# Gathering expert tokens from two 4-byte parts instead of three bf16 parts

## The reference, cut to what matters

```
scores = sigmoid(t @ w_router);  sel = scores + e_bias
... (only the 4 best of 8 groups of experts stay in sel)
_, eidx = lax.top_k(sel, TOP_K)                      # 8 of 64
w = take_along_axis(scores, eidx);  w = w / sum(w) * 2.5
hg = einsum('cd,edf->cef', xc, w_eg);  hu = einsum('cd,edf->cef', xc, w_eu)
a  = silu(hg) * hu * gates[..., None]
routed = einsum('cef,efd->cd', a, w_ed)
shared = (silu(t @ w_sg) * (t @ w_su)) @ w_sd
```

## Time and profile before

| | |
|---|---|
| median of 3 runs | 1138.94 us |
| the profiled execution | 1141.19 us |
| its span | 1139.4 us |
| TensorE busy | 1086.8 us (95%), 7070 instructions |
| weight loads | 749.6 us (66%) |
| VectorE, ScalarE busy | 381.0 us (33%), 274.0 us (24%) |
| bytes moved | 334.45 MB, mean 294 GB/s |

### The profile page before, as it was taken

One profiled execution on the slowest core, in us unless ns is written; L12 is line 12 of the kernel. 1 busy time (PEld: TensorE's weight loads), 2 busy tenths in 40 slices (PEclk: granted clock), 3 DMA queues, 4 the chain that ended last, 5 costly groups with the idle time before them and its releaser, 6 DMA issues.

```text
span 1139.4 us, 17633 instructions
## 1 busy us (share of the span) xinstructions
PE 1086.8 (95%) x7070; PEld 749.6 (66%) x7070; DVE 381.0 (33%) x975; ACT 274.0 (24%) x614; POOL 52.7 (5%) x85
## 2 busy tenths in 40 slices
PE   6999999999999999999899999999699999999998
PEld 4786875688755455555555556544278888887567
DVE  1398966442613111111121121112033111341941
ACT  2124135501511111112111110111023121212951
POOL 0000202104000000000000000000001001100001
PEclk9999999999999999999999999999799999999999
DMA  9999378945689999999999999999964344210000
GB/s 387 345 421 422 123 322 349 418 160 188 246 304 414 414 416 417 416 416 421 416 420 415 416 419 413 414 418 415 415 276 146 111 144 151 74 38 1 1 1 37
DMA packets 59074, 334.45 MB, mean 294 GB/s; under 512 B 6608, under 2 KB 7984, under 8 KB 28784
## 3 DMA queue, kind: packets, MB, share of 16 engines
q1 hardware_dynamic: 56592, 327.97, 71.4%
q10 hardware_dynamic: 2176, 3.37, 1.0%
q0 software_dynamic: 224, 1.97, 0.4%
HBM read 332.23 MB, written 1.05 MB: 293 GB/s over the span
## 4 chain that ended last, share of the span: by engine, by line
PE 78%; DMA 12%; DVE 4%; SPq 3%; issue 2%; ACT 1%; DVEq 0%; ACTq 0%
DMA ring<-experts 12%; PE bank L1036 11%; PE bank L523 10%; PE bank L1080 5%; PE bank L1171 5%; PE bank L987 4%; PE bank L905 4%; PE bank L430 3%; PE bank L926 3%; PE bank L1272 2%; PE bank L815 2%; PE bank L1223 2%; PE bank L830 2%; PE bank L653 2%; PE bank L589 2%; PE bank L961 2%
## 5 line engine op out<-in xcount | busy, mean ns | idle before, releaser
L1036 PE MATMUL bank<-ring,arena 128*32 128x512 f32 (+1 forms) x1120 | 182.2, 625 | 20.2 <-DMA ring<-experts 19.9
L1036 PEld LDWEIGHTS bank<-ring,arena 128*32 128x32 f32 (+1 forms) x1120 | 53.0, 124 | 131.0 <-issue 130.8
L523 PE MATMUL bank<-hT,ring 128*128 128x256 f32 x576 | 126.9, 381 | 0.0
L523 PEld LDWEIGHTS bank<-hT,ring 128*128 128x128 f32 x576 | 109.0, 190 | 18.2 <-issue 4.0
L1080 PE MATMUL bank<-ring,arena 128*32 128x512 f32 (+1 forms) x560 | 87.6, 597 | 1.7 <-DMA ring<-experts 1.7
L905 PE MATMUL bank<-arena 128*128 128x128 bf16 x1152 | 72.2, 219 | 1.1 <-ACT arena L1632 1.1
L905 PEld LDWEIGHTS bank<-arena 128*128 128x128 bf16 x1152 | 66.9, 98 | 7.9 <-issue 5.0
L2247 DVE TENSOR_TENSOR yhalf<-bank,yhalf 128x512 fp32r<-128x512 f32 x48 | 33.2, 692 | 92.0 <-ACT yhalf L1659 92.0
L2234 DVE SCALAR_TENSOR_TENSOR arena<-bank,arena 128x256 f32<-128x256 f32 x24 | 11.6, 484 | 151.1 <-ACT arena L1651 147.1
L1403 POOL TENSOR_TENSOR hT<-hT 128x256 f32<-128x256 f32 x30 | 21.7, 724 | 852.4 <-ACT hT L1460 851.0
L1171 PE MATMUL bank<-hT,ring 128*128 128x256 f32 x256 | 57.1, 379 | 0.0
(11 more groups left out here) (372 smaller groups left out, 1462.4 us busy)
## 6 DMA issues: line engine op xcount, KB each, us to landing
ring<-stream SPq DMA_DIRECT2D x118, 1024.0 KB, 12.0
ring<-experts SPq DMA_DIRECT2D x114, 1024.0 KB, 17.1
ring<-experts SPq DMA_DIRECT2D x156, 512.0 KB, 14.8
arena<-consts POOLq DMA_DIRECT2D x1, 1664.0 KB, 12.1
resid<-x SPq DMA_DIRECT2D x1, 1024.0 KB, 5.0
resid<-ctx ACTq DMA_DIRECT2D x1, 1024.0 KB, 10.1
arena<-stream SPq DMA_DIRECT2D x1, 1024.0 KB, 11.4
bias_room<-rpb ACTq DMA_DIRECT2D x2, 438.0 KB, 5.5
```

What stands on the lines that cost most here:

```text
L523: mm = mmul(o[:, 0:n_tok], w[:, k, t * P:(t + 1) * P], hT[:, k, 0:n_tok], start=(k == 0), stop=(k == KT - 1))
L1036: mm = mmul(o[at:at + n_slots, :], xg[:, kk, at:at + n_slots], w[g][:, k, :], start=(kk == 0), stop=(kk == KT - 1))
```

## The change

The tokens are split in two parts in the 4-byte single-pass format (`hparts`): ScalarE writes the first from PSUM, VectorE the difference. `htok`, the second and third parts are gone. The gather has 8 x 2 x 2 = 32 instructions a unit. `choose` writes the choice twice, as bf16 (for the gate and scatter products) and as F32R (`chosen_r`). VectorE computes ranks and the sorted list directly after the mask, then the two last rests, then the gates; `ordered` is signalled by the copy itself. TensorE does 5 of 8 k-steps of the first `shu` tile ahead of the sorted list, the others and the second tile behind it and ahead of `by_expert`. The sorted list uses bank 7 instead of 3, the second `shu` tile bank 5 instead of 1. To make room, the first 4096 columns of the arena become a room of their own that is used by early tiles, then by `hparts`, `chosen_r`, `yhalf` and `selT`, then by late tiles.

```diff
+        with nc.sbuf_tensor("early_room", [P, FRONT + 512 + 8 * RUN + 1024], F32) as early_room:
...
+        with nc.sbuf_tensor("hparts", [P, 2, 2, 1024], F32R) as hparts:
+            pass
+        late_room = sb("late_room", [P, FRONT])
...
+        chosen_r = sb("chosen_r", [P, 2, 2, P], F32R)
...
-            shu_tile(0, 6)
+            shu_part(0, 6, range(0, 5))
             pe.wait_ge(S("perm_made"), 1)
-            o = open_group("order", 3)
+            o = open_group("order", 7)
             mmul(o[0:1, 0:64], cc("expert")[0:64, :], perm, start=True, stop=True)
             close_group(mmul(o[0:1, 64:128], count_col, perm, start=True, stop=True), "order")
+            shu_part(0, 6, range(5, KT))
+            shu_part(1, 5, range(KT))
+            slab_end[nu] = ("shu", 1)
             pe.wait_ge(S("gates_made"), 1)
-            done(pe, "pos")
             o = open_group("by_expert", 2)
...
-            shu_tile(1, 1)
-            slab_end[nu] = ("shu", 1)
 
             def gather(m, half):
 
                 o = open_group(("xg", m, half), 4)
                 if half == 0:
                     pe.wait_ge(S("chosen_made"), m + 1)
+                if m == 0:
+                    done(pe, ("tk", half))
+                    done(pe, ("tk", 2 + half))
                 for d in range(4 * half, 4 * half + 4):
                     for t in range(TT):
-                        for q in range(3):
-                            mm = mmul(o[:, P * (d % 4):P * (d % 4) + P], hbf[:, q, t, P * d:P * d + P],
-                                      chosen[m % 2][:, t, :], start=(t == 0 and q == 0), stop=(t == 1 and q == 2))
+                        for q in range(2):
+                            mm = mmul(o[:, P * (d % 4):P * (d % 4) + P], hparts[:, q, t, P * d:P * d + P],
+                                      chosen_r[:, m % 2, t, :], start=(t == 0 and q == 0), stop=(t == 1 and q == 1))
...
             def first_part(gg):
                 full(act, ("tk", gg))
-                a.copy(hbf[:, 0, gg // 2, 512 * (gg % 2):512 * (gg % 2) + 512], bk(("tk", gg))[:, :]).then_inc(S("part_a"), 1)
-
-            def second_part(gg):
-                act.wait_ge(S("rest_a"), gg + 1)
-                a.copy(hbf[:, 1, gg // 2, 512 * (gg % 2):512 * (gg % 2) + 512], htok[:, gg % 2, :]).then_inc(S("part_b"), 1)
+                a.copy(hparts[:, 0, gg // 2, 512 * (gg % 2):512 * (gg % 2) + 512], bk(("tk", gg))[:, :]).then_inc(S("part_a"), 1)
...
             def rest_of(gg):
                 dve.wait_ge(S("part_a"), gg + 1)
-                v.tensor_tensor(htok[:, gg % 2, :], bk(("tk", gg))[:, :], hbf[:, 0, gg // 2, 512 * (gg % 2):512 * (gg % 2) + 512],
-                                ALU.subtract).then_inc(S("rest_a"), 1)
-
-            def third_part(gg):
-                dve.wait_ge(S("part_b"), gg + 1)
-                at = hbf[:, :, gg // 2, 512 * (gg % 2):512 * (gg % 2) + 512]
-                emptied(v.tensor_tensor(at[:, 2, :], htok[:, gg % 2, :], at[:, 1, :], ALU.subtract), ("tk", gg))
+                at = hparts[:, :, gg // 2, 512 * (gg % 2):512 * (gg % 2) + 512]
+                emptied(v.tensor_tensor(at[:, 1, :], bk(("tk", gg))[:, :], at[:, 0, :].bitcast(F32), ALU.subtract), ("tk", gg))
...
-            link(v.tensor_tensor(gates, lg, mask, ALU.mult))
-            link(v.tensor_reduce(den[:, 2:4], gates, AXX, ALU.add))
...
-            for gg in range(2):
-                third_part(gg)
-                done(dve, ("tk", gg))
-                rest_of(gg + 2)
-            third_part(2)
-            third_part(3)
+            link(v.memset(order[0:1, E:E + 1], 0))
+            v.tensor_tensor(gates, lg, mask, ALU.mult)
             full(dve, "pos")
...
+                for to in (chosen[m % 2], chosen_r[:, m % 2]):
+                    if kind == "X":
...
             choose(0)
             full(dve, "order")
-            link(v.memset(order[0:1, E:E + 1], 0))
-            v.tensor_copy(order[0:1, 0:E], bk("order")[0:1, 0:64])
+            v.tensor_copy(order[0:1, 0:E], bk("order")[0:1, 0:64]).then_inc(S("ordered"), 1)
             emptied(v.tensor_copy(count_rank, bk("order")[0:1, 64:128]), "order")
-            done(dve, "order")
-            signal("ordered")
+            rest_of(2)
+            rest_of(3)
+            link(v.tensor_reduce(den[:, 2:4], gates, AXX, ALU.add))
...
```

More of the change, by code:

```diff
@@ L150, in build, with cut @@
         rstd = sb("rstd", [P, 512])
[L151 to L155, removed]
+        arena = sb("arena", [P, ARENA - FRONT])
+        def cut(room, at, n, dims, parts=P):
+            v = room[0:parts, at:at + n]
             if len(dims) == 2:
@@ L160, in ar, with early, late @@
             return v
+        def ar(at, n, *dims, parts=P):
+            return cut(arena, at - FRONT, n, dims, parts)
+        with nc.sbuf_tensor("early_room", [P, FRONT + 512 + 8 * RUN + 1024], F32) as early_room:
+            def early(at, n, *dims):
+                return cut(early_room, at, n, dims)
+            stat = early(FRONT, 512)
+            braw = early(FRONT + 512, 8 * RUN, 8, RUN)
+            bmask = early(FRONT + 512 + 8 * RUN, 1024, 2, 512)
+            wr = early(FRONT + 512, 512, 8, 64)
+        with nc.sbuf_tensor("hparts", [P, 2, 2, 1024], F32R) as hparts:
+            pass
+        late_room = sb("late_room", [P, FRONT])
+        def late(at, n, *dims):
+            return cut(late_room, at, n, dims)
+        chosen_r = sb("chosen_r", [P, 2, 2, P], F32R)
+        yhalf = sb("yhalf", [P, 2, 1024], F32R)
+        selT = sb("selT", [P, 2, P], F32R)
+        sb("rest_of_early_room", [P, 8 * RUN + 1536 - 2816])
         def cc(name, a=0, b=None):
@@ L169, in vv @@
             return ve[:, lo + a:(hi if b is None else lo + b)]
-        qk = ar(0, 2048, 8, 256)
-        vna = ar(2048, 1024, 2, 512)
-        lat = ar(3072, 1024, 4, 256)
+        qk = early(0, 2048, 8, 256)
+        vna = early(2048, 1024, 2, 512)
+        lat = early(3072, 1024, 4, 256)
         sgate = ar(4096, 4096, 16, 256)
@@ L281, in build @@
         rt2 = ar(9216, 1024, 4, 256)
-        outs = ar(0, 2048, 2, 1024)
+        outs = late(0, 2048, 2, 1024)
         gdiag = hT[:, :, T:T + P]
[L285 to L290, removed]
         bank = [ctx.enter_context(nc.psum_tensor(f"bank{b}", [P, 512], F32)) for b in range(8)]
@@ L1102, in more_tokens @@
                         for t in range(TT):
-                            for q in range(3):
-                                mm = mmul(bank[4][:, P * (d % 4):P * (d % 4) + P], hbf[:, q, t, P * d:P * d + P],
-                                          chosen[0][:, t, :], start=(t == 0 and q == 0), stop=(t == 1 and q == 2))
+                            for q in range(2):
+                                mm = mmul(bank[4][:, P * (d % 4):P * (d % 4) + P], hparts[:, q, t, P * d:P * d + P],
+                                          chosen_r[:, 0, t, :], start=(t == 0 and q == 0), stop=(t == 1 and q == 1))
                     mm.then_inc(S("more_on_tensor"), 1)
@@ L2138, in choose @@
                 kind, ranks_of = UNITS[m]
[L2139 to L2149 removed]
+                for to in (chosen[m % 2], chosen_r[:, m % 2]):
+                    if kind == "X":
+                        for r, at, n_slots in ((ranks_of[0], 0, 96), (ranks_of[1], 96, 32)):
+                            src = ranked[:, :, r:r + 1]
+                            last = v.tensor_tensor(to[:, :, at:at + n_slots], bc(cc("iota"), [0, 2], [1, n_slots]),
+                                                   bc(src, [src.ap[1][0], 2], [0, n_slots]), ALU.is_equal)
+                    else:
+                        G = len(ranks_of)
+                        W = P // G
+                        src = ranked[:, :, ranks_of[0]:ranks_of[0] + G] if m else first2
+                        last = v.tensor_tensor(to.rearrange("p t (g w) -> p t g w", g=G), bc(cc("iota"), [0, 2], [0, G], [1, W]),
+                                               bc(src, [src.ap[1][0], 2], [1, G], [0, W]), ALU.is_equal)
                 last.then_inc(S("chosen_made"), 1)
@@ L2153, in _ @@
             full(dve, "order")
-            link(v.memset(order[0:1, E:E + 1], 0))
-            v.tensor_copy(order[0:1, 0:E], bk("order")[0:1, 0:64])
+            v.tensor_copy(order[0:1, 0:E], bk("order")[0:1, 0:64]).then_inc(S("ordered"), 1)
             emptied(v.tensor_copy(count_rank, bk("order")[0:1, 64:128]), "order")
-            done(dve, "order")
-            signal("ordered")
+            rest_of(2)
+            rest_of(3)
+            link(v.tensor_reduce(den[:, 2:4], gates, AXX, ALU.add))
+            link(v.reciprocal(den[:, 2:4], den[:, 2:4]))
+            for t in range(TT):
+                last = v.tensor_scalar(gates[:, t, :], gates[:, t, :], den[:, 2 + t:3 + t], 2.5, ALU.mult, ALU.mult)
+            last.then_inc(S("gates_made"), 1)
             full(dve, "by_expert")
```

44 lines of the change are left out of this document (13 added, 31 removed).

## The result

The changed kernel took 1145.96 us, the median of 3 runs (1145.64 to 1146.42), against 1138.94 before. The ratio is 1.0057, with a 95% interval of 1.0039 to 1.0076. It is slower, by 7.0 us or 0.6%, where 1.7 us were forecast. Its profiled execution took 1145.64 us 4.45 more than the profiled one of before; its span is 1143.8 for 1139.4. In a later session, with 10 runs of the changed kernel and 31 of the one before, the ratio was 1.0034 (1.0017 to 1.0050).

A forecast was written before the change was run, and what follows sets the result against it. The transfer stream, full from 359.5 to 838 us, was taken to set the expert stage's end. Work ahead of unit 0, -0.83, and three gathers, +2.55, gave +1.7 us: 1140.7 us, range 1136.5 to 1151 for 8 in 10.

The forecast's parts named there:

- The gather: Each unit's gather on TensorE: 32 4-byte instructions at 0.110 us for 48 bf16 at 0.056, +0.85 us a unit.
- loads and streams in turn: Rival for the gather: 4-byte loads and streams don't overlap, up to 0.166 us an instruction, 1148 to 1175; chance 0.17.
- two passes: Rival for the gather: two loads a product, 0.22 us each, +78 us, about 1217; chance 0.09.
- a price per instruction: Rival for the gather: load hidden, 0.056 us an instruction, -0.88 us a unit, 1135.5; chance 0.10.
- Ahead of unit 0: Reordered work before the first gather: TensorE starts that gather at 308.14 instead of 308.97, -0.83 us.
- The first restart: Transfer stream's restart at 335.57, after two units' gathers: -0.83 + 2 x 0.85 = +0.9 us.
- The second restart: Transfer stream's restart at 358.57, after three units' gathers: -0.83 + 3 x 0.85 = +1.7 us, all counted.
- The head start: Four slabs asked for 2.5 us sooner through the earlier order; only lengthens the pause at 332.5, priced 0.
- that rival: The early order pays: the 2.5 us head start survives the pause at 332.5, 1136.4 to 1138.2; chance 0.09.
- After 359.5: Expert stage's 21 remaining gathers: +17.9 us of TensorE's work, covered by its waits; the last slab still ends the stage.
- The reserve: TensorE's waits over the rest of the expert stage, about 21.6 us, taken as cover for the later gathers.
- VectorE and the overlays: Second choice, 0.4 to 0.5 us a unit on VectorE, hidden by a 2.68 us wait; overlays add nothing: 0.

The follow-up runs named there:

- The filled kernel: Changed kernel with three k-steps of the shared expert's second up tile between the first gather's halves; 1141.08 us, and 1141.01 us when run again.
- the order alone, e1: Kernel before, three bf16 parts and 48 instructions kept, with only the changed order of work ahead of unit 0; 1139.33 us, ratio 0.9996.
- after_again: The changed kernel unaltered, run again in a later session; 1144.94 us, ratio 1.0034 to the kernel before.
- e3: Changed kernel with units 3 to 23 gathered from the first part alone, units 0 to 2 unchanged; 1141.75 us, ratio 1.0022.
- e2: Changed kernel with units 0 to 2 gathered from the first part alone, 16 instructions each instead of 32; 1138.34 us, ratio 0.9977.
- e4_fill: Changed kernel with three k-steps of the shared expert's second up tile between the first gather's halves; 1141.08 us, ratio 1.0016.
- e4_fill_again: The e4_fill kernel run a second time, no edit; 1141.01 us, ratio 1.0008.
- e10: The e4_fill kernel with all context steps half a unit later; 1158.63 us, ratio 1.0170.
- e6: The e1 kernel with the first part added a second time, so 64 bf16 gather instructions a unit; 1141.94 us, ratio 1.0013.
- e5: The e1 kernel with three k-steps of the shared product between the first gather's halves; 1140.23 us, ratio 0.9997.
- e7: The e5 kernel with all context steps one unit later, none left in unit 0; 1142.64 us, ratio 1.0016.
- e9: The e5 kernel with all context steps half a unit later; 1154.23 us, ratio 1.0112.

## Why the prediction was right and wrong

The mechanism was right as far as it went: slower gathers, covered by the waits behind the restart and paid ahead of it. 1145.96 lies in the range of 1136.5 to 1151, but that is partly luck. The forecast's own 1139.5 to 1142.5 was missed, the value of 1140.7 was 5.3 us too low, and the range went up to 1151 for a dearer gather, which did not come. What brought the time up there was a fall of the clock that the sum did not have. By its steps:

- **The gather.** 0.110 us an instruction was forecast, 0.112 is the median distance of starts; 32 x 0.112 - 2.67 = +0.91 us a unit for +0.85. The loads last 192 ns (188 to 192 said), a half 1.97 to 2.10 us. The rivals of loads and streams in turn (from 0.116 on), of two passes (0.22) and of a price per instruction (0.056) are all out. The row to trust was L787, the 4-byte loads alone. The Trainium skill, TensorE: Matmul & The Clock Gate, section "LDWEIGHTS (loading the stationary operand)", puts a load at its columns over 1.2 in ns, 107 for 128. The 0.112 from start to start agrees within 5% for this format, the 0.056 of the bf16 gather does not; a single load's record is longer in both, 192 and 98 ns.
- **Ahead of unit 0.** -0.83 was forecast, -0.66 came. TensorE did not wait for the permutation, the counts start at 300.96 for 303.34 on VectorE, and the first ordered issue comes 2.4 us earlier.
- **The first restart.** +0.9 was forecast, +4.65 came. The step that failed is not a wait or a price but the clock in unit 0: 6.8 us at 1.2 GHz, 3.4 us lost. The prediction looked at the granted clock only behind long waits at the end of the stage and took unit 0's products at their old duration. The filled kernel, twice, gives 4.4 us back and keeps the gathers; what remains, +0.24, is -0.66 + 1.82 - 0.77 = +0.39 within 0.15.
- **The second restart.** The sum counted three gathers, because the transfers had run low at 357. It should have counted two. In ten traces the last down product follows the first restart by 478.3 to 480.3 us. After against before it is 4.08 us later against the router, with the first issue 4.65 and the second 5.5 later. That alone lies within the spread of 2.0 us. The rates decide: at the second issue the stream moves 324 GB/s for 417 over 2.5 us before and 376 over 5 us after, so it loses an estimated 0.6 and 0.5 us there, as much in one kernel as in the other. By the same steps with two gathers and the measured price, -0.66 + 1.82 = +1.2 was the sum to make, and the clock's 3.4 the term that was missing. The third gather, 0.85 too much in the sum, hid a part of that.
- **The head start** was priced at 0, and in the order alone the issues come 2.4 us earlier and the restart 0.2. Right; that rival is out.
- **After 359.5.** The reserve took the 21 gathers: 7.8 us of waits are left (3 to 8 said), 4.02 of them at the last gate and up products, where 2.3 was said. With 37.6 us of TensorE's work taken away, the last down product moved by 0.7.
- **VectorE and the overlays** were priced at 0. VectorE is busy 386.5 us for 381.0, and TensorE has no wait for it from 303 to 842 us.

The 4.4 us between the spans of the profiled executions are all accounted for: the router 0.42 later, the restart 4.65, what follows it -0.57, the rest -0.10. The medians are 7.0 us apart in the first session and 5.2 in the later one. The profiled execution of before was 2.25 us above its median and the changed kernel's 0.32 below, which is the difference to 7.0; single executions of before lie between 1137.4 and 1144.0. The intervals of both ratios, 1.0039 to 1.0076 and 1.0017 to 1.0050, hold 4.45 us (the first at its lower end), so no loss beyond it is shown.

## What to carry to other kernels

When a transfer stream is the bound, find the last point at which it stood still: only TensorE's work ahead of that point is paid. A dip behind it is no such point when the stream loses little there (0.5 us here). When instructions are replaced by fewer and slower ones, price them by a row of the same load, and then read the granted clock of the stretch behind them, as sparse products with a wait of one microsecond between them may halve it for what comes next. A few independent products moved into that wait are worth more than the wait itself: 4.4 us for 0.98 here.

## What the runs showed of the hardware that was not expected

**The clock fell with TensorE busy.** The granted clock at 312 to 322 us, over all thirteen traces:

```
gather                       wait between its halves   clock
4-byte, 0.112 us each        0.98 us                   1.2 GHz for 6.8 us (after, after_again, e3)
4-byte, 16 a unit            0.98 us                   1.2 GHz for 3.4 us (e2)
4-byte, 0.112 us each        filled                    2.4 GHz (e4_fill, e4_fill_again, e10)
bf16, 0.056 us each          0.77 to 1.03 us           2.4 GHz (before, e1, e6)
bf16, 0.056 us each          filled                    2.4 GHz (e5, e7, e9)
```

Neither the wait nor the 4-byte gather does it alone. Nor does the place in time: the second half of the gather starts 23.81 us behind the router in e2, with the fall, and at 23.43 in e4_fill and 24.86 in e6, without. That the array has less to do in a product that mostly waits for its weights fits this, but no run measured that.

**A wait behind the last down product.** TensorE's timeline after, and beneath it the row of before, at the end of the expert stage:

```profile
827.25 9.57 PE L1164 MATMUL bank<-ring,arena 128*128 128x512 f32 x16 [3.97 <-issue]
```

```profile
822.70 9.65 PE L1147 MATMUL bank<-ring,arena 128*128 128x512 f32 x16 [3.92 <-issue]
```

In the eleven other traces that wait is 3.73 us to none, and the step from the last down product to this one is 5.1 to 8.1 us, 7.6 in these two. It is the same in both, so it is no part of the change. From the last down product to the end of the span takes 320.1 to 324.3 us over the thirteen, so single executions lie up to 4 us apart behind that point. Its cause stays open.
